# Turning a finished query block later, and copying it on ScalarE instead of VectorE

## The reference, cut to what matters

```python
def block(i):
    start = i * Q_BLOCK
    qpos = start + jnp.arange(Q_BLOCK, dtype=jnp.int32)
    score = _indexer_scores(sl(qi), sl(wi), ki, qpos, kpos)
    _, idx = lax.top_k(score, topk)
    return _sparse_attend(sl(q), _gather_rows(k, idx), _gather_rows(v, idx), qpos, idx, rel_bias)
```

## Time and profile before

| what | value |
|---|---|
| median of 3 runs | 1483.9 us (1478.82 to 1487.71) |
| time of the profiled execution | 1484.16 us |
| its span | 1482.5 us |
| PE, DVE, ACT, POOL busy | 93%, 45%, 33%, 17% of the span |
| mean granted clock of PE | 0.966 |
| the 34 steps of the loop | about 680 to 831 us |

### The profile page before, as it was taken

One profiled execution on the slowest core, in us unless ns is written; L12 is line 12 of the kernel. 1 busy time (PEld: TensorE's weight loads), 2 busy tenths in 40 slices (PEclk: granted clock), 3 DMA queues, 4 the chain that ended last, 5 costly groups with the idle time before them and its releaser, 6 DMA issues. The chain is left out here.

```text
span 1482.5 us, 28944 instructions
## 1 busy us (share of the span) xinstructions
PE 1381.0 (93%) x11422; PEld 1294.3 (87%) x11422; DVE 663.5 (45%) x1129; ACT 494.0 (33%) x716; POOL 251.8 (17%) x305
## 2 busy tenths in 40 slices
PE   6999999999988999949899888879999999999996
PEld 5999999999986778837888776669999999999996
DVE  4333233434461239747897422226543433343344
ACT  5332222212240321235677333223432222222244
POOL 4000000388005000213467312200000000000000
PEclk8999999999998999969999999979999999999998
DMA  9522222332233552172122669661233322223221
GB/s 131 159 83 76 86 85 85 93 93 82 80 111 47 102 105 70 16 133 77 48 63 78 217 206 326 202 204 58 85 88 94 88 86 85 85 85 94 84 65 61
DMA packets 231059, 152.62 MB, mean 103 GB/s; under 512 B 29986, under 2 KB 212074, under 8 KB 230971
## 3 DMA queue, kind: packets, MB, share of 16 engines
q1 hardware_dynamic: 203392, 121.40, 28.8%
q0 software_dynamic: 7088, 19.65, 5.4%
q10 hardware_dynamic: 20490, 10.36, 3.1%
HBM read 141.85 MB, written 8.34 MB: 101 GB/s over the span
## 5 line engine op out<-in xcount | busy, mean ns | idle before, releaser
L1755 DVE TENSOR_TENSOR w_low<-wraw,w_high 128x1024 fp32r<-128x1024 f32 x144 | 179.6, 1248 | 319.6 <-ACT w_high L1259 319.5
L1259 ACT ACTIVATE w_high<-wraw 128x1024 fp32r<-128x1024 f32 x144 | 152.5, 1060 | 443.0 <-PE ps L637 438.4
L637 PE MATMUL ps<-hn_high,w_high 128*128 128x272 f32 x1408 | 292.6, 289 | 2.9 <-DVE w_low L1755 2.9
L637 PE MATMUL ps<-hn_high,w_low 128*128 128x272 f32 x1408 | 292.4, 289 | 0.0
L637 PE MATMUL ps<-hn_low,w_high 128*128 128x272 f32 x1408 | 291.3, 288 | 0.0
L637 PEld LDWEIGHTS ps<-hn_high,w_high 128*128 128x128 f32 x1408 | 222.6, 189 | 3.1 <-issue 3.0
L637 PEld LDWEIGHTS ps<-hn_low,w_high 128*128 128x128 f32 x1408 | 222.3, 189 | 0.0
L637 PEld LDWEIGHTS ps<-hn_high,w_low 128*128 128x128 f32 x1408 | 220.8, 190 | 0.0
L637 PE MATMUL ps<-act_high,w_high 128*128 128x272 f32 x832 | 173.1, 289 | 3.3 <-DVE act_low L1755 1.8
L637 PE MATMUL ps<-act_high,w_low 128*128 128x272 f32 x832 | 171.9, 288 | 0.0
L637 PE MATMUL ps<-act_low,w_high 128*128 128x272 f32 x832 | 171.6, 288 | 0.0
(11 more groups left out here) (362 smaller groups left out, 1812.9 us busy)
## 6 DMA issues: line engine op xcount, KB each, us to landing
wraw<-in_w_ffn_in SPq DMA_DIRECT2D x88, 512.0 KB, 3.9
wraw<-in_w_ffn_out SPq DMA_DIRECT2D x32, 512.0 KB, 3.9
wslot<-in_w_in SPq DMA_DIRECT2D x16, 512.0 KB, 4.0
wraw<-in_w_ffn_out SPq DMA_DIRECT2D x16, 384.0 KB, 3.5
wslot<-in_w_in SPq DMA_DIRECT2D x4, 1024.0 KB, 5.4
wslot<-in_w_s_glu SPq DMA_DIRECT2D x16, 256.0 KB, 3.0
biasmem<-in_cache_k SPq DMA_DIRECT2D x16, 256.0 KB, 4.0
wslot<-in_w_in ACTq DMA_DIRECT2D x8, 512.0 KB, 5.8
```

What stands on the lines that cost most here:

```text
L637: ins = pe.matmul(ps[:, bank + h, 0:HALF], a[:, w_at, k, :], x[:, lo_at(k) if x is x_lo else k, h * HALF:(h + 1) * HALF], start=(k == 0 an ...
L1259: act_e.activation(wh[:, j % 2, :, :], wraw[:, j, :, :], ACT.Copy).then_inc(s["hi_done"], 1)
L1755: return dve.tensor_tensor(o, a, b, op)
```

## The change

`p_turn_out` of blocks 0, 1 and 2 moves from the end of step x = 9, 17, 25 on PE to the middle of step x = 10, 18, 26: behind the scores and the first `tile_half`, ahead of `p_turn`. For block 3 it stays where it was, after the last values. The copy to `attT` leaves DVE's queue and enters ACT's, at the same steps behind the copy of the turned probabilities and ahead of `tile_high`; for block 3 it stands after ACT's loop, ahead of the two `ga_load` issues. DVE no longer waits for `att_turned` at the end of a block, save the old wait for the buffer of `ao`.

```diff
@@ PE, the loop
                     tile_half(x, 0)
+                if x >= 3 and (x - 3) % 8 == 7:
+                    p_turn_out((x - 3) // 8)
                 if 1 <= x < 33:
                     p_turn(x - 1)
                 if x < 32:
                     tile_half(x, 1)
                 if x >= 2:
                     p_values(x - 2)
-                if x >= 2 and (x - 2) % 8 == 7:
-                    p_turn_out((x - 2) // 8)
+            p_turn_out(3)
             pe.wait_ge(s["evac"], EV0 + ALLT)
@@ ACT, ahead of its loop
+            def att_turn_out(qb):
+                act_e.wait_ge(s["att_turned"], qb + 1)
+                if qb == 0:
+                    act_e.wait_ge(s["kv_out"], 16 * 4)
+                act_e.activation(attT[:, :, P * qb:P * qb + P], ps[:, 6, :].rearrange("p (j n) -> p j n", j=4), ACT.Copy).then_inc(s["att_out"], 1)
+
@@ ACT, in its loop and behind it
                     act_e.activation(pT[:, (x - 1) % 2, 0:w], ps[:, 3, 0:w], ACT.Copy).then_inc(s["probs_out"], 1)
+                if x >= 3 and (x - 3) % 8 == 7:
+                    att_turn_out((x - 3) // 8)
                 if x >= 2 and x % 2 == 0 and x // 2 + 1 < SPLIT:
                     tile_high(x // 2 + 1)
                 if x in (3, 5, 7, 9):
                     act_e.activation(gT_high[(x - 3) // 2][:], gT[:, (x - 3) // 2, :], ACT.Copy).then_inc(s["rhs_high"], 1)
+            att_turn_out(3)
+
@@ DVE, the end of a block
-                    dve.wait_ge(s["att_turned"], qb + 1)
-                    if qb == 0:
-                        dve.wait_ge(s["kv_out"], 16 * 4)
-                    dve.tensor_copy(attT[:, :, P * qb:P * qb + P], ps[:, 6, :].rearrange("p (j n) -> p j n", j=4)).then_inc(s["att_out"], 1)
```

## The result

The changed kernel took 1468.28 us in the median of 4 runs (1464.42 to 1472.33), beside 1485.19 us for the kernel before in 4 runs (1478.82 to 1487.71): a ratio of 0.9894 (95% interval 0.9859 to 0.9930). The profiled execution of the changed kernel took 1464.42 us with a span of 1462.7, so it is the fastest of its four, and 19.8 us shorter in span than the profiled one of before.

The account below looks back on a forecast made before the run. PE was taken to bound the stage, with its four stops reachable: 4.57 + 1.35 + 1.22 + 0.7 = 7.8 us, so 1484.16 - 7.8 = 1476.3 us. The range was 1472.0 to 1480.5 us.

Parts of the forecast that it names:

- the end: Block 3: DVE computes the mask beside the transposes, ACT copies, and PE starts the mask's matmul earlier; gain 0.7 us.
- How the numbers follow: Step setting chances, predicted time 1476.3 us and range 1472.0 to 1480.5 from the forecast and its rivals.
- best case: Rival that PE's clock also stays up after block 3's stops: gain 9.4 us, 1474.8 us; chance 0.18.
- the smaller gains: Two rivals: clock falls at block 0 (1479.0 us, chance 0.16) or DVE becomes the bound (1478.6 us, chance 0.11).
- The scale of the sum: Step subtracting gains from one execution of 1484.16 us, 0.3 us above the median of the runs shown.
- The remaining wait at block 0: Block 0: DVE's order ahead of the scaling is unchanged, so at least 2.0 us of PE's wait stay.
- DVE follows: Block 0: DVE starts its next maximum 2.3 us earlier and uses 2.16 us idle time, keeping pace with PE's 4.57 us.
- DVE becomes the bound: Rival: DVE can't use its idle 2.16 us, holding PE to 2.3 us at block 0; gain 5.6 us, chance 0.11.
- ACT's copy is hidden: Before the next block's first values: ACT's 0.60 us copy finishes with 0.3 us to spare, about 0.1 at block 2.
- falls at block 0 all the same: Rival: PE works at 1.2 GHz after block 0's remaining 2 us stop, losing 2.6 us; gain 5.2, chance 0.16.
- Further up: Rival: shorter stops at block 3 keep PE's clock at 2.4 GHz, saving 1.6 us more; gain 9.4, chance 0.18.
- 7.8 us earlier: Sign at the loop's end: the mask's matmul should start about 7.8 us earlier than 831.70.

Follow-up runs that it names:

- before_late: Kernel before, with ACT's first two weight roundings moved behind the sample index's relus and bias copies: 1486.82 us, ratio 1.0026 to the kernel before.
- before_quiet: Kernel before without the two stores of the prompt's k and v: 1481.96 us, ratio 0.9985 to the kernel before.
- c_before: Kernel before once more, unchanged: 1478.92 us in 12 runs, ratio 0.9986 to the same kernel.
- act_only: Kernel before with only ACT's half: copy by ACT for all four blocks, turning where it was: 1480.61 us, ratio 0.9995 to the kernel before.
- pe_only: Kernel before with only PE's half: turning half a gate tile later, copy still by DVE: 1470.08 us, ratio 0.9934 to the kernel before.
- c_after: Changed kernel once more, no edit: 1471.08 us in 12 runs, ratio 0.9952 to the kernel before.
- after_quiet: Changed kernel without the two stores of the prompt's k and v: 1471.38 us, ratio 0.9922 to the kernel before.
- c_after2: Changed kernel a third time, no edit: 1472.52 us in 12 runs, ratio 0.9944 to the kernel before.
- scale_first: Changed kernel with DVE's reciprocal and scaling ahead of its top-k rounds of the same step: 1469.87 us, ratio 0.9909 to the kernel before.
- scale_copy: Changed kernel with DVE's scaling ahead of its top-k rounds and, at block steps, ACT's two copies ahead of the exponential: 1471.36 us, ratio 0.9914.
- the late pair: before_late and after_late: both kernels with ACT's first two weight roundings behind the sample index's work; 1486.82 and 1474.33 us.
- the quiet pair: before_quiet and after_quiet: both kernels without the stores of the prompt's k and v; 1481.96 and 1471.38 us.
- after_late: Changed kernel with ACT's first two weight roundings behind the sample index's relus and bias copies: 1474.33 us, ratio 0.9930 to the kernel before.

## Why the prediction was right, and where it was wrong

**The mechanism and its size.** Between the same instructions after gains 10.09 - 5.48 = 4.61 us at block 0 (predicted 4.57), 4.80 - 3.37 = 1.43 at block 1 (1.35), 5.12 - 3.83 = 1.29 at block 2 (1.22), and 0.5 to 0.7 at the end (0.7): 2.14 to 1.62 or 1.40. Together 7.8 to 8.0 us; the sum was 7.8. The runs of both kernels behind the first comparison say the same: 98 of before have a mean of 1481.5 us, 24 of after 1473.4, a difference of 8.1 us, plus or minus 3.1 (95%). So the mechanism and its size held, and 1468.28 was missed for another reason.

**The step that failed** is in "How the numbers follow": the range allowed 2.8 us below its best case and 1.5 above the smaller gains as "some of the scatter of single runs". It had three runs of before within 9 us, and took one execution near their middle, 1484.16, as the level ("The scale of the sum"). Neither the level nor the scatter was sized from enough runs. The 98 runs have a standard deviation of 6.0 us and reach from 1468.30 to 1494.16; the 24 of after 7.2 us, 1461.25 to 1484.31. A mean of four such runs has an error of about 3 to 3.6 us, a median somewhat more, and the difference of two such sets about 4.7. The forecast missed 1468.28 by some 8 us: 2.6 because 1484.16 lies above the 98 runs' mean, 5.1 because the four runs of after lie below the mean of its 24, and 0.3 in the size of the change. The interval of the first comparison, 0.9859 to 0.9930, was too narrow as well: the repeats gave 0.9952 and 0.9944. That both sets of four lay apart by chance is the simplest reading of the 9 us beyond the change, but it is not shown to be the whole one: four and four runs drawn at random from the 98 and the 24 give medians 16.9 us or more apart in about 6 of 100 draws (an estimate from these runs).

For the profiled pair the trace gives the bill of the 19.8 us of span: 8.4 in "ahead", 7.4 in the four blocks, 0.5 at the end, and the other 3.5 elsewhere: 4.2 gained between the mask's matmul and matmul 8000, 0.7 behind that, and 1.4 lost before "ahead". The prediction set what a measurement can tell at 7.4 us; that fits dozens of runs, not four.

**Where those 8.4 us are.** PE waits in L988 for ACT, ACT waits for the weights of its first two roundings (16.2 us before, 2.3 after, in the two profiles, 640 to 690 us), and the DMA rate in this stretch has two values in the same kernel. before_late shows that the wait travels with the roundings; before_quiet shows that the k and v stores don't make it. What sets the rate stays open. One trace of it that no run tested: from 640 to 665 us the same 2.10 MB of ACT's loads (`biasmem<-scr_shift`) took 55.7% of the 16 DMA engines' time in before and 27.7% in after. Of the profiles in which ACT's roundings stand where they were, the four with the turning at its old place all have the long value (29.1 to 31.0 us: before, c_before, act_only, before_quiet). Of the seven with the turning moved, three have it (pe_only, c_after, after_quiet), three the short one (after, c_after2, scale_first, 21.9 to 22.0) and scale_copy 25.4. That is too few to exclude that the change shifts the odds, though nothing of it runs there; the 5.0 to 11.2 us of the pooled interval leave room for it, and the late pair (12.9 us) and scale_first (12.2) point that way, while c_after (7.3 by means, on its chip), c_after2 (8.8) and the quiet pair (8.4) don't. Whether the change is worth more than its 7.8 us outside the blocks stays open.

**The remaining wait at block 0**: predicted 2.0 us, 2.33 measured, DVE's order unchanged as said. The first part of the stop went to the scores and the half tile.

**DVE follows** by using its idle 2.16 us, as argued from the earlier trace rows; no idle time before the maxima of 717.90 and 720.87. The rival "DVE becomes the bound" is out for the change. In scale_copy PE does wait for DVE, 1.4 us at the scores.

**ACT's copy is hidden**: 593 to 597 ns for the four, predicted 598 from the earlier trace rows, with 0.43, 0.33 and 0.22 us to spare against 0.3 to 0.1 predicted. The same copy stands in both kernels, on DVE before and on ACT after (count, then ns min/median/max):

```profile
L2103 DVE COPY kvtok<-ps x4: 691/692/692, 721.8 to 830.3; 128x512 f32<-128x512 f32 x4
L1526 ACT ACTIVATE kvtok<-ps x4: 593/594/597, 714.8 to 816.0; 128x512 f32<-128x512 f32 x4
```

The Trainium skill (ScalarE: Activation LUTs, Rules for kernel authors) gives `relu`, `max`, `min`, `add` and `mul` to VectorE, with up to about 3 times its speed per element in bf16, and doesn't name a copy; for this copy, fp32 out of PSUM, ACT was the faster one by 0.10 us. What spoke against the move was not ACT's speed but its queue: scale_first shows the price, 2.49 us at one block, when the exponential ahead of the copy comes late.

**The clock.** At block 0 it stayed at 1.00 in after, c_after, c_after2 and pe_only, and fell in after_late and after_quiet: the rival "falls at block 0 all the same" is real in some executions. It was priced at 2.6 us, with the fall before the transposes, and cost 1.5 (34.9 against 33.4), because the clock fell only behind `p_turn`: values to `p_turn` at block 0 still took 5.58 and 5.49 us in these two. "Further up" was not seen in the changed kernel: behind the loop PE works at 0.50 in each profile, and in after for longer (815.4 to 825.6) than in the profile of before (831.7 to 835.2). But c_before has it from 835.4 to 845.6, so this length too differs between executions of one kernel. The pooled difference can't tell 1.5 us in either direction.

**The end.** The loads behind ACT's copy landed in 3.8 to 10.2 us, 6.3 in the median, and the first was in time. Of the predicted "7.8 us earlier" for the mask's matmul, the profiles show 831.70 - 816.68 = 15.0 us, because the time ahead of the loop lies in it; the four blocks' stretches (115.5 to 108.1) and the end (0.5) give 7.9. The rest lies ahead of the blocks.

## What to carry to other kernels

A stop that repeats at the end of each block is best priced by following one instruction to the next across the stop, in PE's order, and by asking what of the wait stays when the work is moved into it: here 2.3 of 4.7 us. Before a gain of half a percent is compared with a measurement, look at how far executions of the unchanged kernel lie apart; four runs of each showed twice the gain here, while the time between the same two matmuls in the traces gave it to tenths. Where the change reorders the work, follow the instruction, not its number. Work moved onto another engine is held by what is queued ahead of it there, not by its own duration: look at the releaser of the instruction in front of it.

## What the runs showed of the hardware

The DMA engines of a core, fully busy with the same kernel's transfers at the same place, moved 142 to 155 GB/s in one execution and 250 to 262 in another; the loads of the two weight tiles landed in 21.0 us in the median in the first (c_after) and 6.7 in the second (after). What sets the rate was not found. Whether a stop of 2.3 us of PE was followed by the low clock differed between executions too, at the same instructions: clock 1.00 in four profiles, 0.56 to 0.59 in two. A copy of 128x512 fp32 values out of PSUM took 593 to 597 ns on ACT and 691 to 692 on DVE.
